# Inside and around eight RWKV head pairs on one Trainium2 core: GpSimd's masks get two more waits, and the steps before and after the pairs are put in another order

## The reference, cut to what matters

```python
def second_block(x, c, ctx, ...):
    px = modulate(rms_norm_2(x, norm_mix[i]), sh1, sc1) @ w_in[i]
    pc = modulate(rms_norm_2(xc, norm_mix[i]), csh1, csc1) @ w_in[i]
    yc_rw, s_ctx = rwkv_mix(rwkv_streams(conv3(pc[..., :RW_COLS], rw_shift[i]), *rw_args), (s_zero, s_zero), *out_args)
    yx_rw, _ = rwkv_mix(rwkv_streams(conv3(px[..., :RW_COLS], rw_shift[i]), *rw_args), s_ctx, *out_args)
    yx = jnp.concatenate([yx_rw, short_conv_mix(px, conv_w[i], grid_conv3), fourier_mix(px)], axis=-1) @ w_out[i]
    x = x + ga1 * yx
    x = x + ga2 * ffn(modulate(rms_norm_2(x, norm_ffn[i]), sh2, sc2), w_gate[i], w_up[i], w_down[i])
def wkv_scan(r, w, k, v, kk, a, s0, reverse):          # once forward, once backward in time
    def step(s, inp):
        sa = jnp.einsum('bhij,bhj->bhi', s, -kk_t)
        s = s * w_t[:, :, None, :] + sa[..., None] * (kk_t * a_t)[:, :, None, :] + v_t[..., None] * k_t[:, :, None, :]
        return s, jnp.einsum('bhij,bhj->bhi', s, r_t)
def rwkv_mix(streams, s0, ln_w, ln_b, r_k, g_up):
    ...                                                # the two scans, a norm per head, a bonus
    g = jax.nn.sigmoid(gd) @ g_up                      # the gates
    return y.reshape(b, l, D_RWKV) * g, (sf, sb)
def fourier_mix(p):
    y = jnp.fft.fftn(u, axes=(1, 3), norm='ortho').real
```

## Time and profile before

| | us |
|---|---|
| median of 3 runs | 3294.78 |
| lowest, highest | 3293.04, 3303.99 |
| the profiled execution | 3302.67 |
| its span in the trace | 3300.9 |
| its pairs stage, from the end of the input projection to the start of the output projection | 1790 to 2312.5 |

### The profile page before, as it was taken

One profiled execution on the slowest core, in us unless ns is written; L12 is line 12 of the kernel. 1 busy time (PEld: TensorE's weight loads), 2 busy tenths in 40 slices (PEclk: granted clock), 3 DMA queues, 4 the chain that ended last, 5 costly groups with the idle time before them and its releaser, 6 DMA issues.

```text
span 3300.9 us, 69277 instructions
## 1 busy us (share of the span) xinstructions
PE 3064.2 (93%) x32062; PEld 2754.8 (83%) x32062; DVE 1559.1 (47%) x2216; ACT 573.3 (17%) x1058; POOL 1217.0 (37%) x709
## 2 busy tenths in 40 slices
PE   5998998998999999999899788897999999999998
PEld 4877887877887888788698677776989999999998
DVE  4655276446337720378851577676245441113111
ACT  2022202011120020200001555553010000000001
POOL 2000010000000001135285444442648897777774
PEclk8998999998999999999999899999999999999999
DMA  7965288766226635367842000000545654444442
GB/s 277 416 242 181 103 318 318 274 259 238 109 103 241 244 126 201 128 229 287 306 184 104 8 7 9 7 6 28 193 154 225 249 194 175 170 163 154 160 175 100
DMA packets 55920, 583.07 MB, mean 177 GB/s; under 512 B 7202, under 2 KB 9568, under 8 KB 10704
## 3 DMA queue, kind: packets, MB, share of 16 engines
q1 hardware_dynamic: 38080, 466.11, 37.7%
q0 software_dynamic: 17552, 112.54, 9.0%
HBM read 576.52 MB, written 2.10 MB: 175 GB/s over the span
## 4 chain that ended last, share of the span: by engine, by line
PE 73%; DVE 11%; DMA 9%; issue 3%; POOL 2%; ACT 1%; SPq 0%; ACTq 0%; DVEq 0%; POOLq 0%
PE PS L1708 24%; PE PS L374 15%; PE PS L672 7%; DMA ring<-in_w_vec_dram 5%; PE PS L1661 5%; DMA ring<-in_w_second_dram 2%; DVE ring L2298 2%; PE PS L1890 2%; PE PS L417 2%; DMA ring<-in_w_start_dram 1%; PE PS L371 1%; PE PS L1909 1%; PE PS L1833 1%; PE PS L1725 1%; DVE ring L888 1%
## 5 line engine op out<-in xcount | busy, mean ns | idle before, releaser
L374 PE MATMUL PS<-H,ring 128*128 128x256 f32 x2944 | 669.2, 386 | 7.0 <-ACT H L702 7.0
L374 PEld LDWEIGHTS PS<-H,ring 128*128 128x128 f32 x2944 | 562.4, 193 | 95.0 <-issue 17.6
L1708 PE MATMUL PS<-H,ring 128*128 128x128 f32 x3424 | 404.4, 276 | 4.6 <-DMA ring<-in_w_second_dram 4.6
L1708 PEld LDWEIGHTS PS<-H,ring 128*128 128x128 f32 x3424 | 394.4, 193 | 5.4 <-DMA ring<-in_w_second_dram 5.0
L327 POOL DMA_DIRECT2D ring<-in_w_vec_dram x75 | 39.7, 530 | 923.2 <-DVE ring L888 785.0
L2405 DVE TENSOR_TENSOR W<-W,PS 128x256 f32<-128x256 f32 x58 | 24.4, 421 | 676.9 <-ACT W L2044 676.8
L1708 PE MATMUL PS<-H,W 128*128 128x128 f32 x2624 | 314.6, 275 | 4.2 <-POOL W L1537 3.8
L1708 PEld LDWEIGHTS PS<-H,W 128*128 128x128 f32 x2624 | 303.3, 192 | 5.1 <-POOL W L1537 4.6
L1532 POOL TENSOR_TENSOR W<-ring 128x1024 f32<-128x1024 f32 (+1 forms) x74 | 182.4, 2464 | 260.9 <-PE PS L1708 149.6
L672 PE MATMUL PS<-H,ring 128*128 128x256 f32 x1024 | 223.5, 379 | 2.9 <-DVE H L1174 2.9
L672 PEld LDWEIGHTS PS<-H,ring 128*128 128x128 f32 x1024 | 194.2, 190 | 29.9 <-issue 3.7
(11 more groups left out here) (496 smaller groups left out, 4987.6 us busy)
## 6 DMA issues: line engine op xcount, KB each, us to landing
ring<-in_w_second_dram SPq DMA_DIRECT2D x97, 2048.0 KB, 8.2
ring<-in_w_first_dram SPq DMA_DIRECT2D x68, 2048.0 KB, 8.4
ring<-in_w_vec_dram POOLq DMA_DIRECT2D x75, 1024.0 KB, 7.8
ring<-in_w_vec_dram SPq DMA_DIRECT2D x48, 1024.0 KB, 5.0
ring<-in_w_start_dram SPq DMA_DIRECT2D x16, 2048.0 KB, 15.7
H<-in_w_vec_dram POOLq DMA_DIRECT2D x21, 1024.0 KB, 8.0
Pj<-in_w_aside_dram SPq DMA_DIRECT2D x8, 2048.0 KB, 11.2
ring<-in_w_second_dram SPq DMA_DIRECT2D x9, 1536.0 KB, 6.6
```

Source lines behind the costliest of these rows:

```text
L374: mm = pe.matmul(PS[:, t % 2, half * T:(half + 1) * T], ring[:, t % 2, k, half * P:(half + 1) * P], hT[:, k, :], start=(k == 0), stop=(k = ...
L1708: mm = pe.matmul(regions(bank2, r), w[:, k * P:(k + 1) * P], m[:, k, :], start=(first and k == 0 and r // 4 not in opened), stop=(last and ...
```

## The change

- **Masks.** GpSimd's level 2 masks wait for both `p_x0` of the pair; its level 5 masks wait for the first `p_cs` of the next pair.
- **Copies of the scores.** ScalarE's `below` copies `aT` for both directions first, then `br` for both.
- **Pair 0.** VectorE's `stream` now takes a direction; for pair 0 VectorE does both, and GpSimd's `stream_back(0)` is gone.
- **Start.** The Fourier tiles come ahead of the convolution tiles in `WIN2`. TensorE's first transform waits only for tile 20's banks, gives `ft_1` per half, and uses banks 0 to 3; its second goes half by half into banks 4, 5, 0, 1. ScalarE's copies between them go to `ring` slot 2, so GpSimd's wait for `mix_rest` and VectorE's for `mix_ft` are gone. Tanh and Sigmoid move to after tile 16. ScalarE copies the transform into `mix` after `keys(0)`. On TensorE `key_sums(0)` comes ahead of the gates, and the gates stand between the decays.
- **End.** The first output tile goes to slot 1, and its load waits for `p_ypre` of pair 7 in place of `p_y`. Its chunks 0 to 6 wait for the end of pair 6, and only the last chunk for that of pair 7.

```diff
-WIN2 = [KV0 + TW * i for i in range(8)] + [WD0] + [TW * i for i in range(4)] + [GD0] + [CG0 + TW * i for i in range(6)] \
-    + [FT0 + TW * i for i in range(2)]
+WIN2 = [KV0 + TW * i for i in range(8)] + [WD0] + [TW * i for i in range(4)] + [GD0] + [FT0 + TW * i for i in range(2)] \
+    + [CG0 + TW * i for i in range(6)]
...
-SLOT = [q % 2 if q < NIN2 else (q - NIN2) % RING for q in range(len(SECOND))]
+SLOT = [q % 2 if q < NIN2 else (q - NIN2 + 1) % RING for q in range(len(SECOND))]
...
-    CG, CX, CB, FT = Pj[:, 42:46, :], Pj[:, 46:50, :], Pj[:, 50:54, :], Pj[:, 54:58, :]
+    FT, CG, CX, CB = Pj[:, 42:46, :], Pj[:, 46:50, :], Pj[:, 50:54, :], Pj[:, 54:58, :]
+    ft_banks = (4, 5, 0, 1)
...
             if q == Q_OUT[0]:
+                sp.wait_ge(S("p_ypre").sem, S("p_ypre").at(NP2, 0))
+            if q == Q_OUT[1]:
                 sp.wait_ge(S("p_y").sem, S("p_y").at(NP2, 0))
...
-        pool.wait_ge(S("mix_rest").sem, 4)
...
                 need("p_P", j, count(lev - 1, d))
+                if lev == 2:
+                    need("p_x0", j, 2)
+                if lev == 5 and j < NP2 - 1:
+                    need("p_cs", j + 1, 1)
...
-            need("p_streams" if j else "p_kk", j, 1)
+            need("p_streams", j, 1)
...
         pool.wait_ge(S("cells_loaded").sem, 16)
-        stream_back(0)
...
-        for q in Q_OUT[0:2]:
-            pe.wait_ge(read_sig(q).sem, read(q))
-        need(S("mod_done"), 1)
-        for tt in range(TT):
+        pe.wait_ge(read_sig(Q_OUT[0]).sem, read(Q_OUT[0]))
+        for s, name in enumerate(("dft_c", "dft_s")):
+            for tt in range(TT):
+                for i in range(4):
+                    mm = pe.matmul(PS[:, 2 * s + tt, i * P:(i + 1) * P], FT[:, i, tt * P:(tt + 1) * P], Dc(name), start=True, stop=True)
+            done(mm, "ft_1")
+        pe.wait_ge(read_sig(Q_OUT[1]).sem, read(Q_OUT[1]))
+        for s, name in enumerate(("seq_c", "seq_s")):
+            need(S("ft_copied"), s + 1)
             for i in range(4):
-                pe.matmul(PS[:, 4 + tt, i * P:(i + 1) * P], FT[:, i, tt * P:(tt + 1) * P], Dc("dft_c"), start=True, stop=True)
-                mm = pe.matmul(PS[:, 6 + tt, i * P:(i + 1) * P], FT[:, i, tt * P:(tt + 1) * P], Dc("dft_s"), start=True, stop=True)
-        done(mm, "ft_1")
-        need(S("ft_copied"), 2)
-        for i in range(4):
-            for s, name in enumerate(("seq_c", "seq_s")):
                 for tt in range(TT):
-                    mm = pe.matmul(PS[:, i, 0:T], flat(W[:, 4 * s:4 * s + 4, :])[:, tt * 512 + i * P:tt * 512 + (i + 1) * P],
+                    mm = pe.matmul(PS[:, ft_banks[i], 0:T], flat(RG[:, 32 + 4 * s:36 + 4 * s, :])[:, tt * 512 + i * P:tt * 512 + (i + 1) * P],
...
         def pairs_ended(n, k):
-            if n == 8:
-                pe.wait_ge(S("pair_end").sem, S("pair_end").at(NP2, 0))
+            if n in (8, KC - 1):
+                pe.wait_ge(S("pair_end").sem, S("pair_end").at(NP2 if n > 8 else NP2 - 1, 0))
...
+        key_sums(0)
         pe.wait_ge(S("gate_loaded").sem, 16)
-        pe.wait_ge(S("lora_act").sem, S("lora_act").start + 2)
+        pe.wait_ge(S("mix_ft").sem, S("mix_ft").start + 2)
         gates(0)
+        need("p_kms", 0, 1)
+        decays(0, 0)
         gates(1)
-        key_sums(0)
-        need("p_kms", 0, 1)
-        for d in range(2):
-            decays(0, d)
+        decays(0, 1)
+        gates(2)
         key_norms(0)
-        gates(2)
...
+            if n == 17:
+                act.wait_ge(read_sig(Q_IN[16]).sem, read(Q_IN[16]))
+                do(f(WA[0:LORA, 0, :, :], WA[0:LORA, 0, :, :], ACT.Tanh), S("lora_act"))
+                do(f(GD, GD, ACT.Sigmoid), S("lora_act"))
             act.wait_ge(tiles_done.sem, multiplied(q))
             if 1 < n < 14:
                 need(S("in_conv"), n - 1 if n < NWIDE else n - 3)
             do(f(in_result(n)[:, 3, :], in_regions(n % 2, n < NWIDE, 0), ACT.Copy), S("ff_first"))
-        for q in Q_OUT[0:2]:
-            act.wait_ge(read_sig(q).sem, read(q))
-        do(f(WA[0:LORA, 0, :, :], WA[0:LORA, 0, :, :], ACT.Tanh), S("lora_act"))
-        do(f(GD, GD, ACT.Sigmoid), S("lora_act"))
-        need(S("ft_1"), 1)
         for s in range(2):
-            do(f(W[:, 4 * s:4 * s + 4, :].rearrange("p (t a) b -> p t (a b)", t=2), PS[:, 4 + 2 * s:6 + 2 * s, :], ACT.Copy), S("ft_copied"))
-        need(S("ft_2"), 1)
-        do(f(mix[:, 12:16, :], PS[:, 0:4, 0:T], ACT.Copy), S("mix_ft"))
-        pairs_act(act)
+            need(S("ft_1"), s + 1)
+            do(f(RG[:, 32 + 4 * s:36 + 4 * s, :].rearrange("p (t a) b -> p t (a b)", t=2), PS[:, 2 * s:2 * s + 2, :], ACT.Copy), S("ft_copied"))
+
+        def fourier():
+
+            need(S("ft_2"), 1)
+            for n in range(2):
+                do(f(mix[:, 12 + 2 * n:14 + 2 * n, :], PS[:, ft_banks[2 * n]:ft_banks[2 * n] + 2, 0:T], ACT.Copy), S("mix_ft"))
+        pairs_act(act, fourier)
...
                 f("p_aTc", aT[d].rearrange("p (r n) b -> p r (n b)", r=2), PS[:, 2 * d:2 * d + 2, 0:T], ACT.Copy)
+            for d in range(2):
...
         keys(0)
+        fourier()
...
-        need(S("mix_ft"), 1)
-        for n in range(3):
-            do(v.memset(sm[:, 90 + n:91 + n], 0.0), S("mix_rest"))
-        do(v.memset(GS[0][:, 0, :], 0.0), S("mix_rest"))
+        settle()
...
-        def stream(j):
+        def stream(j, d=0):
             o = Order(v, own, j)
-            need("p_tm", j, 1)
-            o.do(v.tensor_tensor(AA[0], AA[0], KK, ALU.mult), S("p_ak"))
-            o.do(v.tensor_tensor(TMP[0], TMP[0], key(j), ALU.mult), S("p_kd"))
-            o.settle()
-            o.do(v.tensor_copy(BN(j).unsqueeze(1), TMP[0][:, 1:2, :]), S("p_bonus"))
-            need("p_exp", j, 1)
-            o.do(v.tensor_tensor(EV[0], EV[0], KK, ALU.mult))
-            need("p_ak", j, 1)
-            o.do(v.tensor_tensor(AA[0], AA[0], EN[0], ALU.mult))
-            o.do(v.tensor_tensor(RT(j, 0).unsqueeze(1), EP[0][:, 1:2, :], rec(j), ALU.mult))
-            o.do(v.tensor_copy(ends(j, 0), flat(EP[0])[:, CH - 1::CH]))
-            o.settle()
-            need("p_kd", j, 1)
-            o.do(v.tensor_tensor(EN[0], TMP[0], EN[0], ALU.mult), S("p_streams"))
+            ak, kd, last = (S("p_akr"), S("p_akr"), S("p_strr")) if d else (S("p_ak"), S("p_kd"), S("p_streams"))
+            need("p_tm", j, d + 1)
+            o.do(v.tensor_tensor(AA[d], AA[d], seq(KK, d), ALU.mult), ak)
+            o.do(v.tensor_tensor(TMP[d], TMP[d], seq(key(j), d), ALU.mult), kd)
+            if d:
+                need("p_akr", j, 2)
+            else:
+                o.settle()
+            if d:
+                o.do(v.tensor_tensor(BN(j).unsqueeze(1), BN(j).unsqueeze(1), TMP[1][:, 1:2, ::-1], ALU.add), ak)
+            else:
+                o.do(v.tensor_copy(BN(j).unsqueeze(1), TMP[0][:, 1:2, :]), S("p_bonus"))
+            need("p_exp", j, d + 1)
+            run = (lambda ins: ins) if d else o.do
+            run(v.tensor_tensor(EV[d], EV[d], seq(KK, d), ALU.mult))
+            run(v.tensor_tensor(AA[d], AA[d], EN[d], ALU.mult))
+            run(v.tensor_tensor(RT(j, d).unsqueeze(1), EP[d][:, 1:2, :], seq(rec(j), d), ALU.mult))
+            o.do(v.tensor_copy(ends(j, d), flat(EP[d])[:, CH - 1::CH]), ak if d else None)
+            if d:
+                need("p_akr", j, 4)
+            else:
+                o.settle()
+            o.do(v.tensor_tensor(EN[d], TMP[d], EN[d], ALU.mult), last)
...
         keys(0)
-        stream(0)
+        for d in range(2):
+            stream(0, d)
```

(3 more changed lines are left out.)

1 line of the change is left out of this document (removed).

## The result

The changed kernel took 3279.02 us in the median of six runs (3276.24 to 3285.28), the kernel before 3302.53 beside it (six runs, 3293.04 to 3306.29). The ratio is 0.9938, interval 0.9924 to 0.9953: faster by 0.62%. A second comparison gave 0.9949 (0.9930 to 0.9969). The forecast of 3265 was 0.991 of the median that it stood on, so about two thirds of the gain came. The profiled execution took 3278.02 us (span 3276.2).

What follows compares the result with a forecast made beforehand. It took the pairs as bound by TensorE's exchange with ScalarE and VectorE, the latter slowed by GpSimd. Gains 11.2 + 4.4 + 9.5 + 4.4 = 29.5 us off 3302.67 give 3273.2, times 0.9976 is 3265; range 3255 to 3279.

Steps and rivals of the forecast that it cites:

- Masks, level 2 (11.2 us): In each pair, GpSimd's masks wait so VectorE's solutions run unslowed; TensorE waits 1.4 us less per pair, 11.2 in all.
- the sign of being wrong: In the pairs: TensorE's unexplained stops growing by as much as its waits shrink would show the forecast wrong.
- Copies (4.4 us): Score copies in the pairs: reordering removes TensorE's wait for ScalarE's copy; 4.4 us taken, bounds 0 and 5.4.
- the supply as a doubt: At the score copies: if instructions arrive at their own pace, the removed wait only becomes more stop; lower bound 0.
- Start (9.5): Before pair 0's scores: earlier key activation and decays, streams on VectorE without GpSimd; 9.5 us, bounds 4.7 and 12.4.
- The clock term: At the start: gates may meet TensorE's 1.2 GHz clock, costing 5.7 us in all; 0.9 of that charged.
- rival A: At the start: clock stays low through the gates; start gives 4.7 us, whole 24.7, so 3270 us; chance 0.18.
- End (4.4): After pair 7: first output tile loads earlier, so TensorE needs no wait for it; 4.4 us, bounds 3.5 and 6.6.
- The level 5 masks: In the pairs: waiting for the next pair's first sums, they are still ready before TensorE asks; nothing gained.
- rival C: In the pairs: level 5 masks come too late and TensorE waits; slower, 3314 us; chance 0.03.
- Rival B: In the pairs: GpSimd is not what slows VectorE, so the masks bring nothing; 18.3 us less gain, 3276; chance 0.08.

## Why the prediction was wrong

- **Masks, level 2 (11.2 us): the step that failed.** What it says of VectorE and of the masks held: 3.13 to 1.29 us, wait 13.1 to 3.0, masks behind the solutions, no wait of TensorE's products for a mask (weight loads waited 3.8 us at level 5 and 1.3 at the others). What failed is "1.4 per pair, 11.2 us": it took a wait on TensorE that vanishes for time gained. The runs without and with it agree within their error (0.9950 and 0.9949), since the stops for instructions grew. From the scores of pair 0 to those of pair 7, TensorE's waits for other engines took 24.5 to 26.0 us in the four profiles without the two edits in the pairs and 11.5 in both with them; its stops took 25.9 to 30.5 and then 36.7 and 39.7. That is the sign of being wrong that the prediction had named, "the unexplained stops growing by as much as the waits shrink"; they grew by about two thirds as much.
- **Copies (4.4 us): failed in the same way.** The text had named the supply as a doubt, with 0 as lower bound, and chose near the top since stops also come where no wait is ahead. That argument does not hold: a pace shows as stops wherever code is dense. And the doubt was put to this term alone, where it bore on the larger one too.
- **Start (9.5): right within the error, by terms that were off to both sides;** 11.2 by runs (7.6 to 14.9), 11.7 between the two profiles. The first key activation is 6.1 earlier against the projection's end (predicted 6.2), the decays 5.4 (6.0). The clock term had the wrong sign. Before, the granted clock was 0.50 from 1812.4 to 1826.0, so the second decays and the key norms of the earlier trace rows had been slow as well, which the sum took as their cost. After, it was 0.50 from 1807.6 to 1810.9 only: the low stretch came, as rival A said, but earlier, at the end of the first gate and on the first decays, and the second decays and key norms ran at the full clock (1.02 and 1.16 us for 2.07 and 2.08). The stream began 8.2 earlier in place of 5.5, and from its start to the scores 3.5 was gained in place of 4.9, in part as an exponential was late (0.69 us).
- **End (4.4): right as far as the runs tell;** 4.3 by runs (0 to 8.6). The load landed in time and the wait of 4.48 is gone. The profiled 7.5 holds 2.6 of clock, which the upper bound of 6.6 did not fully allow.
- **The level 5 masks** cost nothing that shows, so rival C did not come. Rival B had the right size (nothing from the masks) for a wrong reason: GpSimd does slow VectorE.
- **The scale.** The median of three, 3294.78, is low beside 3296.92 to 3302.53 in the later groups; this took a few us off the forecast.
- **Two readings are off, without weight in the sum.** The two slow instructions run from 2084.54 to 2087.67, so they overlap the level 2 masks and do not lie inside them; and 2298.89 and 8.16 add to 2307.05, not 2307.3.

The two profiles by themselves mislead here: the pairs stage took 463.1 us before and 453.4 after, a gain of 9.7. But kernels without the two edits gave 455.2, 457.1 and 459.3 as well; in the profiled run of before three of the eight pairs met a lower clock (0.971 to 0.972), and the rest looks like scatter.

Open is what sets 3.8 us for a packet. In the profile after, the packet behind a stop began 1.0 us or more after TensorE had gone on (median 1.2), took 0.9 to 1.4 (median 1.1), and TensorE went on 1.2 to 1.6 after a packet's end (median 1.4). These make 3.7, as if a packet were asked for only when the block before it is begun; no run tests that. Open is also why fewer instructions gave less than their share.
